# Reversing the column order in which every float32r matmul reads its moving operand and writes its PSUM bank

## The reference

```python
h = x * (1 + scale) + shift
x = layer_norm(alpha * x + gate * mixer_or_ffn(h))
# conv_ffn
u = dwconv_centred(h @ w_up, conv_w, conv_b)      # 1024 -> 5632
gate, val = jnp.split(u, 2, axis=-1)
return (jax.nn.silu(gate) * val) @ w_down          # 2816 -> 1024
```

## Time and profile before

| | before |
|---|---|
| median of 3 runs | 2459.04 us (2454.8 to 2460.25) |
| profiled execution, from first to last instruction | 2459.1 us |
| PE busy | 2342.6 us, 95% |
| DVE busy | 1694.4 us, 69% |
| ACT busy | 1132.1 us, 46% |
| POOL busy | 334.6 us, 14% |
| mean DMA rate | 127 GB/s |
| mean granted TensorE clock | 0.982 of full |

### The profile page before, as it was taken

One profiled execution on the slowest core, in us unless ns is written; L12 is line 12 of the kernel. 1 busy time (PEld: TensorE's weight loads), 2 busy tenths in 40 slices (PEclk: granted clock), 3 DMA queues, 4 the chain that ended last, 5 costly groups with the idle time before them and its releaser, 6 DMA issues.

```text
span 2459.1 us, 35614 instructions
## 1 busy us (share of the span) xinstructions
PE 2342.6 (95%) x13806; PEld 1911.9 (78%) x13806; DVE 1694.4 (69%) x2573; ACT 1132.1 (46%) x1948; POOL 334.6 (14%) x266
## 2 busy tenths in 40 slices
PE   5999999999999999999999998899999999978998
PEld 3765788888888558888878777778888888847998
DVE  2376689987444776999865236768999834486874
ACT  3466554432332666443324444455343325386663
POOL 0000411111100003111112003332111011002110
PEclk8999999999999999999999999999999999999999
DMA  8621645556233022555552420044555636403664
GB/s 255 200 69 58 192 138 163 163 150 203 79 91 94 27 79 78 165 162 158 172 168 72 120 77 27 2 138 119 159 159 161 201 92 122 145 10 112 182 183 132
DMA packets 458426, 312.26 MB, mean 127 GB/s; under 512 B 24258, under 2 KB 413810, under 8 KB 458004
## 3 DMA queue, kind: packets, MB, share of 16 engines
q1 hardware_dynamic: 455488, 308.44, 42.8%
q10 hardware_dynamic: 2772, 1.56, 0.2%
HBM read 308.92 MB, written 1.05 MB: 126 GB/s over the span
## 4 chain that ended last, share of the span: by engine, by line
PE 83%; DVE 7%; ACT 4%; DMA 3%; issue 2%; SPq 1%; DVEq 0%; ACTq 0%
PE bank L1652 72%; PE bank L1945 2%; PE bank L1895 2%; DMA slab_raw<-in_mod_w 1%; PE bank L1915 1%; DVE stat L1281 1%; DVE slab_lo L1015 1%; ACT p L767 1%; ACT hb L586 1%; DMA slab_raw<-in_a_w_o 1%; DVE q_part L1340 1%; PE bank L1726 1%; ACT slab_hi L571 1%; SPq L536 1%; ACT pt L779 1%
## 5 line engine op out<-in xcount | busy, mean ns | idle before, releaser
L1652 PE MATMUL bank<-h_hi,slab_hi 128*128 128x512 f32 (+1 forms) x2416 | 844.3, 349 | 25.5 <-DVE slab_lo L1015 17.9
L1652 PE MATMUL bank<-h_lo,slab_hi 128*128 128x512 f32 (+1 forms) x2416 | 833.9, 345 | 0.0
L1652 PE MATMUL bank<-h_hi,slab_lo 128*128 128x512 f32 (+1 forms) x2416 | 833.6, 345 | 0.0
L1015 DVE TENSOR_TENSOR slab_lo<-slab_raw,slab_hi 128x1024 fp32r<-128x1024 f32 (+1 forms) x388 | 522.7, 1348 | 309.8 <-ACT slab_hi L571 308.6
L571 ACT ACTIVATE slab_hi<-slab_raw 128x1024 fp32r<-128x1024 f32 (+1 forms) x388 | 400.7, 1034 | 313.7 <-PE bank L1652 228.4
L1652 PEld LDWEIGHTS bank<-h_hi,slab_hi 128*128 128x128 f32 x2416 | 463.5, 192 | 102.9 <-issue 42.6
L1652 PEld LDWEIGHTS bank<-h_lo,slab_hi 128*128 128x128 f32 x2416 | 463.9, 192 | 53.2 <-issue 0.5
L1652 PEld LDWEIGHTS bank<-h_hi,slab_lo 128*128 128x128 f32 x2416 | 463.4, 192 | 53.7
L989 ACT ACTIVATE conv<-bank,prm 128x512 f32<-128x512 f32 (+1 forms) x176 | 127.7, 726 | 447.4 <-PE bank L1652 447.3
L1040 DVE SCALAR_TENSOR_TENSOR mod_sum<-slab_raw,cond_wide,mod_sum 128x512 f32<-128x512 f32 x420 | 317.6, 814 | 0.3 <-DMA slab_raw<-in_mod_w 0.3
L1652 PE MATMUL bank<-g_hi,slab_hi 128*128 128x512 f32 (+1 forms) x770 | 268.3, 348 | 2.1 <-ACT res_t L623 2.1
(11 more groups left out here) (242 smaller groups left out, 2657.6 us busy)
## 6 DMA issues: line engine op xcount, KB each, us to landing
slab_raw<-in_ffn_w_up SPq DMA_DIRECT2D x176, 512.0 KB, 3.9
slab_raw<-in_mod_w SPq DMA_DIRECT2D x168, 512.0 KB, 4.6
slab_raw<-in_ffn_w_down SPq DMA_DIRECT2D x64, 512.0 KB, 3.7
slab_gap<-in_mod_w SPq DMA_DIRECT2D x24, 512.0 KB, 7.9
slab_raw<-in_ffn_w_down SPq DMA_DIRECT2D x32, 384.0 KB, 3.2
slab_raw<-in_b_w_qkv SPq DMA_DIRECT2D x24, 512.0 KB, 3.7
slab_raw<-in_c_w_in SPq DMA_DIRECT2D x24, 512.0 KB, 3.8
slab_raw<-in_d_w_qkv SPq DMA_DIRECT2D x24, 512.0 KB, 4.1
```

The source lines that it names most:

```text
L1015: nc.vector.tensor_tensor(wlo[slot][:, 0:w], raw[of][:, 0:w], whi[slot][:, 0:w].bitcast(f32), ALU.subtract).then_inc(s_lo, 1)
L1652: ins = mm(out, l, r, start=first and n == 0, stop=last and n == 2)
```

## The change

Only the call inside `three` changes. The bank slice and the moving operand are both taken with step minus one along the columns, so that the last column is read first and written first; each output column still gets the same value at the same address. The stationary operand, the number of instructions, their order, their waits and all other engines' instructions stay: on each of the five engines, the list of instructions is the same in both kernels (PE 11307 rows, DVE 2121, ACT 1659, POOL 167, SP 595). Two other float32r products, at L1996, don't go through `three` and stay as they are, as do all plain float32 ones.

```diff
             def three(out, w_hi, w_lo, x_hi, x_lo, first, last, moving_w=False):
                 for n, (w, x) in enumerate(((w_hi, x_hi), (w_hi, x_lo), (w_lo, x_hi))):
                     l, r = (x, w) if moving_w else (w, x)
-                    ins = mm(out, l, r, start=first and n == 0, stop=last and n == 2)
+                    ins = mm(out[:, ::-1], l, r[:, ::-1], start=first and n == 0, stop=last and n == 2)
                 return ins
```

## The result

The changed kernel takes 2488.56 us (median of 4 runs, 2482.94 to 2489.27) against 2456.92 us for the kernel before in the same set. The ratio is 1.0125, with a 95% interval of 1.0109 to 1.0141: it is 31 us slower, and clear of the noise. I had forecast no difference.

What follows compares the result with a forecast made beforehand. The prediction took PE's rate of streaming float32r products as the bound. It added 0 for the backward read and 0 for the backward write to 2459.1 us, giving 2459 us, with a range of 2452 to 4215 us.

Steps and rivals of the forecast that it cites:

- What bounds the kernel: Whole kernel: bound by the rate at which PE streams float32r products at L1652, so any price per product lands nearly whole.
- The clock: PE over the whole span: read as at the full granted clock in every slice but the first.
- The write, 0 ns: Products' backward write into PSUM: 0 ns, taken from DVE's backward bank read, 419 ns beside 418 ns forwards.
- The read, 0 ns: Products' backward read of the moving operand from SBUF: 0 ns, taken from ACT rows, 384 ns backwards against 382 ns forwards.
- The fixed 13 ns: Each product at L1652: a fixed part of 13 ns beyond 0.419 ns a column, the same at 512 and 256 columns.
- rival 3: Products at L1652: a smaller price, a pattern's start-up (2592 us) or a stall for part of the columns (about 2900 us); chance 0.15.
- rival 4: Products at L1652: faster, the fixed 13 ns being a write-read conflict that goes, 133 us less, 2326 us; chance 0.02.
- The upper end, a second clock for each column: Every product at L1652 streams one column in two clocks, 1750 us more, 4180 to 4210 us; chance 0.26 as a rival.
- the lower case: In rival 3, one more fixed part of 13 ns for each of 10254 products: 133 us, so 2592 us.
- Faster by the 13 ns: The same claim as rival 4: products at L1652 lose their fixed 13 ns, 2326 us; chance 0.02.

## Why the prediction was wrong

*What bounds the kernel* was right: PE's rate in L1652, with no slack. A price of 6 ns on 6 in 10 of the products (6066 of 10254) came out whole, 33 us by the table with the narrow products' -2 and 31 measured. The clock was read too smoothly: its digit is 9 after the first slice, but it stood at 0.97 between 100 and 235 us. Nothing hangs on it.

*The write, 0 ns*: right, and now shown at PE's own rate (1.0002).

*The read, 0 ns*: this is the step that failed. I took it from ACT's and DVE's rows with a step of minus one, and wrote myself that they run at under half of PE's rate. They are right about ACT and DVE and say nothing on PE. Nor was the step's sign the thing to look for: blocks of 16 with a positive inner step pay the same 6 ns on PE. In its place stands a price of the local order of the moving read, 6.3 ns at 512 columns of h, 5.6 of the slab, 4.4 of g and -1.6 to +3.2 at 256.

*The fixed 13 ns*: mis-read. Two widths with the same remainder looked like a cost of starting a product, and I used it to size both rival 3's start-up price and rival 4. The series show 13 to 23 ns at 512 columns in the forward and backward orders and, by turns from two places, 2.5. All but that 2.5 was a part of the read all along, and there was more to gain in it than the change could lose.

*The upper end, a second clock for each column*: a price of that size exists, but at a step of two (453 ns), not at minus one. So the row of plain float32 products gave about the right size (199 ns read, 214 taken, 227 measured) for the wrong pattern, and it stretched the range to 4215 us. The time lies inside that range only because it was that wide, which is luck and no merit of the reasoning: the time forecast was that of before.

*Rival 3, a smaller price* (0.15) is what happened, with its size a quarter of the lower case (31 us and not 133). Its test, equal growth at both widths for a fixed part or double at the double width for a price per column, was put well, and the answer is neither: +6.3 at 512 and -1.6 at 256 for h.

*Faster by the 13 ns* (0.02, 2326 us): the reason given, the same direction of a last write and a next read, has no support. That a third order of the read comes near its time (2363 us) is a coincidence.

**What stays open.** Why neighbouring columns cost PE 13 to 23 ns a product, why the starts of both operands move it and the stationary operand's width does less, and why two streams are good and four are bad. The runs give the sizes and exclude a load in proportion to the stationary columns, a price per column and one per product. A product without a load of its stationary operand wasn't tried.

## What to carry to other kernels

When PE is the bound, measure the distance between starts against columns / 2.4 and take no remainder as given: here 5% of the dense products' time hung on the order and the start of the moving read, and a short series of products with one setting changed, put where its operands lie ready, prices an order in a few us of one run. Evidence for an access pattern on ACT or DVE isn't evidence for PE. If the activations can be stored so that PE reads two places by turns, price the hopping writes first, and put the odd step on the side of the source rather than of the destination (ACT 888 ns against 1130).

## What the runs showed of the hardware that I had not expected

- A float32r product of 512 columns starts every 226.7 ns with ascending neighbours and both operands from multiples of 128 columns, 233.3 with descending ones or with the stationary operand 4 columns further on, 226.7 again with both 8 columns further on, 215.8 by turns from two places 4 or more columns apart, and 453 with a step of two.
- A backward write of a PSUM bank by PE costs nothing (226.7 ns in a series, 1.0002 in the whole kernel).
- By turns from two places, a product of 320 to 512 columns takes columns / 2.4 + 2.5 ns: 135.8, 162.5, 189.2 and 215.8.
- Below 256 columns, products with 128 stationary columns stay at 111.7 ns in each of the three orders tried (192 and 128 columns alike).
- Directions in alternation cost more than either alone, in the one series that has them: 236.7 ns.
